# A fused transformer stack on one core: the last block's token mixer of tile one placed beside the last tile's expert gathers

## The reference, cut to what matters

```python
proj = h @ w_in                       # 1024 x (4612 + 4096)
(qa, ka, va, qb, kb, vb, qc, kc, vc, f_logit, qd, kd, vd, gate_logit) = split(proj)
log_f = log_sigmoid(f_logit + b_forget);  cum = cumsum(log_f, axis=1)
# per block of 128 queries:
o_a = stick_breaking(qa, ka, va, dist)            # 4 heads of 64
o_b = dilated(qb, kb, vb, slopes)                 # 3 patterns x 4 heads, joint softmax
o_c = forgetting(qc, kc, vc, cum_blk, cum, dist)  # 4 heads, bias cum_q - cum_k
o_d = differential(qd, kd, vd, slopes, lam)       # 4 heads, 2 maps of 32 each
o_d = rms_norm(o_d, diff_g) * 0.8
branch = einsum('bsnc,ncd->bsnd', ys, w_branch)
x = x + sum(sigmoid(gate_logit) * branch, axis=2) @ w_out
```

## Time and profile before

| | us |
|---|---|
| median of three runs | 2439.26 (2436.89 to 2447.5) |
| the profiled execution | 2433.91 |
| its span | 2432.2 |
| TensorE busy in the span | 1874.7 (77%) |
| VectorE busy | 1419.6 (58%) |
| ScalarE busy | 827.8 (34%) |
| granted TensorE clock, mean | 0.887 |

### The profile page before, as it was taken

The page is one execution under the profiler, slowest core; times in us unless marked ns, Lnnn a source line. Parts: engine busy times, 40 slices in busy tenths (PEclk is TensorE's granted clock), DMA queues, the critical chain, the costliest instruction groups (busy, mean ns, idle before and its releaser), DMA issues.

```text
span 2432.2 us, 21025 instructions
## 1 busy us (share of the span) xinstructions
PE 1874.7 (77%) x6722; PEld 1117.0 (46%) x6722; DVE 1419.6 (58%) x2880; ACT 827.8 (34%) x2104; POOL 591.2 (24%) x527
## 2 busy tenths in 40 slices
PE   6686777778778777686787777777769566987988
PEld 3472333623324363232445322222258455866976
DVE  2438845689655569865457974444444266454644
ACT  1211353233425323433522333333334234342532
POOL 0002423343434344442234443333200000000000
PEclk9598988999899889999888999999979655998999
DMA  8067988999999999999799999999834100443542
GB/s 290 30 241 287 406 325 338 421 421 403 394 422 369 368 422 421 385 417 421 263 354 421 421 378 422 421 421 421 357 121 156 54 1 35 174 160 111 184 160 103
DMA packets 103020, 724.84 MB, mean 298 GB/s; under 512 B 12000, under 2 KB 12768, under 8 KB 17152
## 3 DMA queue, kind: packets, MB, share of 16 engines
q0 software_dynamic: 73824, 537.00, 54.0%
q1 hardware_dynamic: 26928, 179.68, 19.5%
q10 hardware_dynamic: 2160, 6.82, 0.7%
HBM read 722.41 MB, written 1.05 MB: 297 GB/s over the span
## 4 chain that ended last, share of the span: by engine, by line
PE 39%; DMA 26%; DVE 20%; ACT 8%; issue 4%; DVEq 1%; POOL 1%; PEldq 0%; POOLq 0%; ACTq 0%; PEld 0%; SPq 0%
DMA sb_work<-in_peer_uv,sb_expert 24%; PE ps_acc L1281 9%; DVE sb_work L1245 5%; PE bank L435 5%; PE bank L497 3%; PE bank L498 3%; PE bank L499 3%; PE bank L1113 3%; PE bank L676 2%; PE ps_acc L498 2%; PE ps_acc L499 2%; PE ps_acc L497 2%; PE ps_turn L373 1%; DVE sb_x L1253 1%; ACT sb_probs L726 1%
## 5 line engine op out<-in xcount | busy, mean ns | idle before, releaser
L1281 PE MATMUL ps_acc<-sb_work,sb_diag 128*128 128x512 f32 x1712 | 875.7, 651 | 284.6 <-ACT sb_diag L1270 246.0
L1840 POOL DMA_INDIRECT sb_work<-in_peer_uv,sb_expert x512 | 586.0, 1145 | 1153.8 <-PE ps_acc L1281 671.6
L1245 DVE CUSTOM_DVE_ANT_0 sb_work<-sb_work,sb_h 128x1024 f32<-128x1024 f32 x512 | 619.0, 1224 | 292.2 <-DMA sb_work<-in_peer_uv,sb_expert 275.4
L1281 PEld LDWEIGHTS ps_acc<-sb_work,sb_diag 128*128 128x128 f32 x1712 | 329.1, 206 | 793.4 <-issue 784.2
L1261 ACT ACTIVATE sb_dots<-sb_dots 128x1 f32<-128x1 f32 x512 | 103.0, 201 | 650.2 <-DVE sb_dots L1245 623.5
L491 DVE TENSOR_TENSOR sb_work_r<-sb_wring,sb_work_r 128x2048 fp32r<-128x2048 f32 (+2 forms) x80 | 168.7, 2130 | 151.2 <-ACT sb_work_r L484 151.2
L484 ACT CAST sb_work_r<-sb_wring 128x2048 fp32r<-128x2048 f32 (+2 forms) x80 | 140.5, 1781 | 115.5 <-PE ps_acc L499 56.8
L1270 ACT ACTIVATE sb_diag<-sb_ident,sb_weight 128x128 f32<-128x128 f32 x428 | 172.2, 402 | 16.4 <-PE ps_acc L1281 2.5
L435 PE MATMUL bank<-sb_wring,sb_hT 128*128 128x512 f32 (+2 forms) x392 | 156.3, 557 | 14.4 <-DVEq L277 5.1
L1262 ACT ACTIVATE sb_weight<-sb_dots,sb_share 128x1 f32<-128x1 f32 x512 | 151.3, 295 | 16.7
L1253 DVE SCALAR_TENSOR_TENSOR sb_x<-sb_work,sb_weight,sb_x 128x1024 f32<-128x1024 f32 x84 | 107.8, 1283 | 60.0 <-ACT sb_weight L1262 59.9
(11 more groups left out here) (259 smaller groups left out, 2037.8 us busy)
## 6 DMA issues: line engine op xcount, KB each, us to landing
sb_wring<-in_peer_w_q SPq DMA_DIRECT2D x32, 1024.0 KB
sb_wring<-in_hyb_w_in SPq DMA_DIRECT2D x20, 1024.0 KB
sb_wring<-in_w_mix SPq DMA_DIRECT2D x18, 1024.0 KB
sb_wring<-in_w_gate SPq DMA_DIRECT2D x16, 1024.0 KB
sb_wring<-in_w_up SPq DMA_DIRECT2D x16, 1024.0 KB
sb_wring<-in_w_down SPq DMA_DIRECT2D x16, 1024.0 KB
sb_wring<-in_mla_w_uq SPq DMA_DIRECT2D x12, 768.0 KB
sb_wring<-in_hyb_w_out SPq DMA_DIRECT2D x8, 1024.0 KB
```

Source lines behind the costliest of these rows:

```text
L1245: e.tensor_tensor_reduce(u, u, h[:, t, :], 1.0, 0.0, ALU.mult, ALU.add, dots[:, i:i + 1]).then_inc(dot_ready, 1)
L1281: last = e.matmul(ps_acc[:, b * 512:(b + 1) * 512], diag[:, number % DIAGS, :], ring[:, n % RING, D + b * 512:D + (b + 1) * 512], start=k ...
L1840: pool.indirect_dma_start(ring[:, n % RING, :], None, a["peer_uv"], bass.IndirectOffsetOnAxis(ap=expert[:, t, n % P:n % P + 1], axis=0)).t ...
```

## The change

Tile one's part of the second model's mixer is written before `finish_experts(1)`, so that its stages carry points for the last tile's items. Tile two's part follows behind. Tile one's products are plain fp32 ones on `hT`, queries and keys made turned already (no `turn` stage); tile two's are plain fp32 ones on a full copy of the turned `h` (`whole`), with queries and keys turned between weight blocks and the running sums after the fourth block in order. The mixing weight is therefore read twice. Masks hold 256 columns, and tile one reads their second half (`of`). They are made by POOL between the fourth and fifth gather of the last tile, and by VectorE in `make_masks`. The forget group comes first, the stick group second. The four forget columns are laid last in the weight and form block 9, used first. Norms, `diff_norm` and the copy of the final norm are per tile; the final norm writes `x` in place. ScalarE's first point of a group now stands behind the stick group's three functions. The three small constants are loaded from SP's queue.

The order of the calls and the new functions, cut (`...` where lines are left out):

```diff
-            for e in ("dve", "act", "pe"):
-                pool.wait_ge(done[e], masks_stage)
+                if n == 3 * P + 4:
+                    for e in ("dve", "act", "pe"):
+                        pool.wait_ge(done[e], mixed_free)
+                    step.add(pool.iota(dist, pattern=[[-1, SEQ]], base=P, channel_multiplier=1,
+                                       allow_small_or_imprecise_dtypes=True))
...
+                    pool.drain().then_inc(masks_made, 1)
...
+        def project_first():
+            turned_of = turned_parts(0)
+            plan = []
+            for b in (9, 0, 1, 2, 3, 4, 5, 6, 7, 8):
+                slots = mix_slots(b)
+                parts = [(products.take(), turned_of[b], [])] if turned_of[b] else []
+                if b in first_rows:
+                    parts.append((products.take(), [], first_rows[b]))
+                for s, _ in slots:
+                    given_back[s] = parts[-1][0].full_at()
+                plan.append((b, slots, parts, point(9.0 if b < 9 else 1.0, "pe")))
...
+        def project_last():
+            turned_of = turned_parts(1)
+            order = (9, 0, 1, 2, 3, 4, 6, 7, 8, 5)
+            by_halves = ()
...
+                        for k in range(4):
+                            start, stop = k0 + k == 0, k0 + k == DC - 1
...
+                                last = e.matmul(u.ap[:, 0:n], whole[:, k0 + k, :], slot_ap(s)[:, k, :],
+                                                start=start, stop=stop)
+                        if j == 0:
+                            last.then_inc(w_used.sem, 1)
+                    last.then_inc(u.full, 1)
+                    if unit:
+                        plan[i - 1][3].wait_emptied(e)
+                        unit.wait_free(e)
...
+                                last = e.transpose(unit.ap[0:width, at:at + P],
+                                                   rows[:, col + c * width:col + (c + 1) * width], ident[:, :])
+                    if i == 3:
+                        forget_pe(e)
...
+        mixed_free = len(stages)
+        finish_experts(0, (1, 1))
+
+        norm(X, X, D, a["final_norm"], [0])
+        norm(X, H, D, a["mix_norm_g_2"], [0])
+        turn_wide(H, hT, DC, [0])
+        make_masks()
+        project_first()
+        forget_first()
+        attend_second(0, scores, first_tmp, first_bias, first_cum)
+        diff_norm(0, True)
+        finish_experts(1)
+
+        norm(X, X, D, a["final_norm"], [1])
+        norm(X, H, D, a["mix_norm_g_2"], [1])
+        turn_split(H, x_pair, [1], whole)
+        project_last()
+        attend_second(1, two_scores, last_tmp, last_bias, last_cum)
+        diff_norm(1)
```

In the act part of `attend`:

```diff
                 for n, g in enumerate(plan):
-                    g["points"][0]("act", e)
...
                         e.activation(az, az, ACT.Ln, bias=1.0).then_inc(from_act.sem, 1)
+                    g["points"][0]("act", e)
```

More of the change, by code:

```diff
@@ L508, in chunk_of, with turn_split @@
             return [q[k // 4][:, k % 4, cols] for q in pair]
-        def turn_split(src, pair):
-            plan = [(t, q, turns.take(), turned_hi.plan()) for t in range(TILES) for q in range(2)]
+        def turn_split(src, pair, tiles=range(TILES), whole=None):
+            plan = [(t, q, turns.take(), turned_hi.plan()) for t in tiles for q in range(2)]
             def pe(e):
@@ L1062, in hybrid @@
                 groups.append(dict(
[L1063 removed]
+                    kind="softmax", tile=t, scale=HD ** -0.5, bias=of(causal, t),
                     maps=[(query(attn_qT, 8 + i), key(i // 2, i, t)) for i in hs],
@@ new lines, in build @@
+        first_hi = work_r[:, 23296:24320].rearrange("p (c s) -> p c s", s=P)
+        x_pair = quads(hT_r[:, :]), quads(work_r[:, 24832:26880])
+        rows = work[:, 8192:8192 + MIX]
+        whole = probsT[:, 0].rearrange("p a b c -> p (a b c)").rearrange("p (c s) -> p c s", s=P)
+        log_f = probsT[:, 1].rearrange("p a b c -> p (a b c)")
+        last_tmp, last_bias = (work[:, 1024 * i:1024 * i + 1024].rearrange("p (n s) -> p n s", n=4) for i in range(2))
+        last_cum = h[:, 1, :].rearrange("p (n s) -> p n s", n=4)
@@ new lines, in build @@
+        masks = mixed[:, :, :].rearrange("p t n -> p (t n)")
+        dist, strict, strict_bias, window, dil_4, dil_16, upper, zero = (masks[:, SEQ * i:SEQ * i + SEQ] for i in range(8))
+        bf = small[:, 0:4]
+        lams = small[:, 8:136].rearrange("p (n d) -> p n d", n=4)
+        cum_q = small[:, 140:148].rearrange("p (t h) -> p t h", t=TILES)
+        diff_gain = small[:, 150:214]
+        forget = small[:, 216:224].rearrange("p (t h) -> p t h", t=TILES)
+        last_landed = sem("last_landed")
@@ new lines, in forget_first, with dve, others, run @@
+        def forget_first():
+            first_dve, act, then_dve, pe, last_dve = forget_parts(
+                0, forget[:, 0, :], products, first_tmp.rearrange("p n s -> p (n s)"), first_cum)
+            p = point(4.0)
+            def dve(e):
+                first_dve(e)
+                then_dve(e)
+                last_dve(e)
+                p("dve", e)
+            def others(part, name):
+                def run(e):
+                    part(e)
+                    p(name, e)
+                return run
+            stage(pe=others(pe, "pe"), act=others(act, "act"), dve=dve, points=[p])
@@ new lines, in masked_slope, with before, forget_bias @@
+        def masked_slope(t, masks, slopes, to):
+            def before(e):
+                link = chains["dve"]
+                link.wait()
+                for i, (m, s) in enumerate(zip(masks, slopes)):
+                    link.add(e.scalar_tensor_tensor(to[:, i, :], of(dist, t), -s, of(m, t), ALU.mult, ALU.add))
+                link.wait()
+            return before
+        def forget_bias(t, cum, to):
+            def before(e):
+                link = chains["dve"]
+                for i in range(4):
+                    link.add(e.scalar_tensor_tensor(to[:, i, :], of(causal, t), cum_q[:, t, i:i + 1], cum[:, i, :],
+                                                    ALU.add, ALU.subtract))
+                link.wait()
+            return before
@@ L1448, in build @@
-        turn(blocks)
-        fl_in, fl_out = to_act.plan(), from_act.plan()
-        l_in, l_out = to_act.plan(), from_act.plan()
-        col_unit = products.take()
-        key_units = [products.take() for _ in range(2)]
-        bf = small[:, 0:4]
-        lams = small[:, 8:136].rearrange("p (n d) -> p n d", n=4)
-        lf_b = stick_tmp[:, :, :].rearrange("p a b -> p (a b)").rearrange("p (r h q) -> p r h q", r=TILES, h=4)
-        cum_q = small[:, 140:148].rearrange("p (t h) -> p t h", t=TILES)
@@ L1538, in build @@
-        masks_stage = len(stages)
-        stage(pe=masks_pe, act=masks_act, dve=masks_dve)
-        def bias_of(t, make):
-            def before(e):
-                for i in range(4):
-                    make(e, i)
-                chains["dve"].wait()
-            return before
-        def masked_slope(t, masks, slopes):
-            w = P * (t + 1)
-            def before(e):
-                link = chains["dve"]
-                link.wait()
-                for i, (m, s) in enumerate(zip(masks, slopes)):
-                    link.add(e.scalar_tensor_tensor(head_bias[:, i, 0:w], dist[:, t, 0:w], -s, m[:, t, 0:w],
-                                                    ALU.mult, ALU.add))
-                link.wait()
-            return before
@@ L1668, in gate_pe @@
                         for k in range(4):
-                            last = product(e, u.ap, chunk_of(x_pair, 4 * i + k, t), [r[:, k, :] for r in right],
+                            last = product(e, u.ap, rows_of(4 * i + k, t), [r[:, k, :] for r in right],
                                            4 * i + k == 0, 4 * i + k == DC - 1)
```

518 lines of the change are left out of this document (319 added, 199 removed).

## The result

The changed kernel took 2383.63 us (median of 4 runs, 2378.41 to 2383.72) against 2439.55 for the kernel before on the same chip: ratio 0.9758, 95% interval 0.974 to 0.9776. A second series of it, beside the last experiments, gave 2385.15 (5 runs, 2380.68 to 2388.96), ratio 0.9772 (0.975 to 0.9794). The forecast was 2378, the range 2348 to 2412. The profiled execution has a span of 2381.9 us, 50.3 less than before; the prediction's sum on that scale was 61 less. On the medians the change is 55.9 us.

The account below looks back on a forecast made before the run. Last tile's gathers bound by DMA bytes, then tail stages the DMA does not limit: -117 behind the gathers, +56 in them, -61 from 2433.91 gives 2373, plus 5 for the median: 2378 us, range 2348 to 2412.

Parts of the forecast that it names:

- The gather stage: Last tile's 128 gathers with tile one's work beside them: 153.1 MB at 402 GB/s, 381 us, +56; bounds +39 and +77.
- The step on the masks: Mask arrays made inside the gather queue: four gathers keep the DMA busy 10 us; 0 taken, 4 left in range.
- The stick step: Tile one's stick group in attention is longer once, some 5 us; eight gather buffers holding 20 us cover most of it.
- rival A: Tile one's attention groups lap as slowly as tile two's did, 22.6 us instead of 17.3: +42, 2420 us; chance 0.12.
- my 17.3: Tile one's attention lap: 14.45 us with 5 items, plus 1.6 items at 1.72 us of TensorE, 17.3 us.
- C: Tile one's projection runs in turns, 26 us a block instead of 17.4: +79, 2457 us; decides from 24; chance 0.06.
- The head: Start of the tail, norms and turning for one tile instead of two: 29 us becomes 17, -12.
- Projection, turning and masks: Tile two's projection by plain products, 78 us, -32; turning and masks leave the tail except 2 us, -39.
- D: Tile two's projection stays at 1.2 GHz: +63 less 3, 2438 us, no change; chance 0.04.
- halves would save 14 us: In tile two's projection, three reduced products instead of a plain one would save some 14 us, by a rule against the change.
- Attention: Tile two's attention alone: 64.7 us plus about 4 for its unhidden start, 68.5 instead of 101.8, -33.
- B: Clock stays up in tile two's attention, joint laps fall from 6.9 to 4.2 us: 2365 us; chance 0.13.

Follow-up runs that it names:

- z1_no_bytes: Changed kernel with tile one's nine wide blocks all reading the same pair of weight slots, leaving out 16.8 MB of mixing weight: 2351.07 us, one run.
- e2_halves: Changed kernel with tile two's nine wide projection blocks as three reduced products of halves instead of plain fp32: 2391.83 us, ratio 0.9797.
- the last kernel: Changed kernel with fuller-filled attention gaps, no drain in the gather queue, and four items inside tile one's forget-gate stage: 2362.91 us, ratio 0.9682.
- f1_gaps: Changed kernel with unused TensorE products filling waits of tile two's attention, none in the joint groups: 2380.29 us, ratio 0.9746.
- f2_gaps_laps: Kernel with filled gaps plus one more unused full-width product in each joint lap: 2388.94 us, ratio 0.9781.
- w1_head: Nine unused TensorE products beside tile two's two norms: last add to first score 90.7 us, against 90.6 in the changed kernel.

## Why the prediction was right, and where it was off

**The sign and the mechanism were right.** The stretch with bytes at its limit grew by less than the tail behind it shrank, and most of what it grew by is bytes. The error on the profiled executions, 11 us of 61, is the first term of the sum, 13 us too small, less 6 won at the projection, with 3 lost at attention, and 2 by which this execution started later. On the medians the change is 5 us nearer to the forecast (55.9): the profiled execution before lay 6 us under its median and the one after on it. That part of the agreement is luck.

**The gather stage, +56 against +69.0.** The mis-sized term is the rate: I took 402 GB/s from the feed beside tile one and it was 388, inside my bounds of 421 and 381 and nearer the lower. The 18.9 MB at 421 are 45 of the 69 (at the price that z1_no_bytes measured, 40); of the other 24 two parts were shown by experiments (5.1 the drain, 4.9 the stick group), a third, 2.9 for the forget-gate stage, rests on its DMA share, and 3.6 are the end, where the last transfer lands near 1821.4 (a share of 0.28 in 1820 to 1825) and the last add comes 10.7 behind it instead of 7.1 before (0.80 in 1750 to 1755, add at 1761.12), since the differential norm stands ahead of the last items. Some 8 us I can't place. The step on the masks failed: I held that four gathers cover the 9.4 us hold and took 0 of a range to 4. The arrays were made at 1440.55 and the hold then took 10.7; by the shares the four transfers ended near 1446.7 and the DMA idled some 5.5 us, of which 5.1 proved to be lost. The stick step (once, some 5 us, and eight buffers that "cover most of it") had the size right and the cover wrong: nothing in the earlier trace rows has a group whose ScalarE and VectorE chain holds the items for so long (7.48 us without a gather on GpSimd), and eight buffers, of which some are being read, did not bridge it.

**Laps and blocks.** 17.1 us a lap against 17.3: rival A (22.6) is out. The mean agrees by chance, though, since it has the stick group in it, which my 17.3 left out. The other six take 16.2, which is the DMA's price of 6.6 items (16.4) and not the TensorE lap that I added up. Tile one's ten blocks took 136.5 us from 1501.3 to 1637.8, some 15 a wide block where I had 17.4; C (26 a block, deciding from 24) is out, and the DMA share was 1.00 all through them: what they waited for was bytes.

**The head, -12.7 against -12:** as worked out.

**Projection, turning and masks, -77.4 against -71.** 73.0 us for the products instead of 78. Eight plain products with nothing between take 0.86 each and the transposes 0.43 a group behind them; I had taken 0.873, 0.136 for a transpose (0.11), a cold start of 2.6 (1.5 lost), and 1.5 for a handover that doesn't show between blocks. D (half clock) is out at a grant of 0.96. That halves would save 14 us is wrong, by e2_halves: they cost 8 to 10, since the splits (1.90 and 2.29 us a megabyte) now stand before the products of one tile only.

**Attention, -30.0 against -33.** The joint laps are 6.89, as forecast. The head of the stage, with no predecessor beside it, is the term mis-sized: 8.0 us from the first score (1922.73) to the stick group's first ScalarE step (1930.76) where I took 4, and 63.9 from there instead of 64.7. B didn't happen, but what it rests on is real: the clock was up at the entry, and 12 us wait there for whoever closes the gaps, which is what the last kernel takes.

**Sign of my own test.** "I am wrong if the DMA falls below 0.9 for long in the gather stage": "for long" had no number. It does for 4 to 16 us at a time, four times, and these places account for some 16 of the 24 us above the bytes.

## What to carry to other kernels

Work moved beside a transfer-bound stretch costs its bytes first (here 45 us for 166 us of work), and then every place where the feeding queue or the consuming engines stop for longer than what is in flight: count buffers that are truly in flight there, not the ring's size. Keep a drain out of the queue that issues the gathers, and signal with a small instruction behind the others. And before pricing a cheaper product form, ask what prepares its operands and when their buffers come back.

## What the runs showed of the hardware that I had not expected

With a drain on GpSimd behind four outstanding gathers the next gather went out 10.7 us after the last array instruction (10.5 to 11.7 in the ten other executions with the drain); a memset in its place let it go 0.46 us after the memset's start. What the drain waits for is not shown: by the share (0.34 in 1445 to 1450) the four transfers ended near 1447, some 4 us before that gather. TensorE's grant does not follow from the work at hand alone: the same joint laps ran at 1.00 throughout with TensorE 91% busy (17.34 of 19 us, f1_gaps) and at 0.50 in the changed kernel, where only the waits ahead of them were not filled. With one wide product more a lap they stayed at 0.50 while 100% busy (18.00 of 18, f2_gaps_laps), whereas the projection's wide products, busy alike, went from half clock to 0.99 at about 1850 (w1_head). Idle TensorE time in the waits of a softmax chain therefore isn't free: 12 us in a stage of 72.
